# Block 2 attention: value products over both token tiles, values projected with stationary weights and turned

## Chip, cores and metric

One core of one Trainium2 chip runs the whole program in one launch. The metric is device time in microseconds (us) of that core. Three executions of the kernel before took 682.45, 682.7 and 682.95 us, median 682.7 us.

## The reference, cut to what matters

Two transformer blocks run one after the other on 256 tokens of width 1024, all in float32. The change touches only the attention of block 2: 8 query heads of 64 columns share 2 key/value heads of 64, the mask is a band of 128 tokens on both sides, there is an ALiBi bias and a sink logit per head.

```python
u = rms_norm_2(h, norm_mix[l])
proj = u @ w_in[l]
z_pool, q, k, v, g_pool, g_attn = jnp.split(proj, splits, axis=-1)
y_pool = multiscale_pool(z_pool, w_pool_group[l], pool_scale[l]) @ w_pool_branch[l]
y_attn = windowed_gqa(q, k, v, sink[l]) @ w_attn_branch[l]
...
p = (p / denom).astype(v.dtype)
out = jnp.einsum("bnhgqk,bnkhd->bnqhgd", p, vb)
```

`v` has 128 columns (2 heads of 64). `out` is the product of the probabilities with the values. After it come the branch products, a merge with two sigmoid gates, the output product, and a gated feed-forward of width 2816.

## The kernel before

Each engine has one instruction list, written out by hand, and runs it in order; the engines meet at counting semaphores (`wait_ge`, `then_inc`). Weights arrive through a ring of eight 1 MB slots by SyncE's queue. A weight slot is used in two parts: ScalarE (ACT) copies it to a rounded high part (`split_high`, line 403, two halves of 1024 columns per slot), VectorE (DVE) writes the rest (`split_low`, line 410), and a product is then three products of reduced-precision operands (`triple`, line 1622: high x high, high x low, low x high). `chunk` (line 1629) makes one 128-column slice of a projection for all 256 tokens: for each of 8 depth tiles it waits for nothing further and issues one `triple`, with the weights stationary and the 256 tokens moving, 24 products in all; before the first it waits for the low half of its slot (`split_ready`). All products are recorded on line 1614 (`mm`), all TensorE transposes on line 1617 (`turn`).

Block 2's projections run in the order pool (4 chunks), query (4 chunks), key (1 chunk, first half of slot `SPLIT1 + 4`), value (second half of that slot). The values are made by `values(i)` (line 2143), once for each of the 2 token tiles: here the 128 tokens of the tile are stationary and the 128 weight columns move, 24 products each, and the result in PSUM bank 6 has tokens on the partitions, as the value products need it. `values(0)` is called before the first scores, `values(1)` after them (line 2194). ACT's `values_out` (line 856) waits for both and copies bank 6 to `v2`, scaled by each token's reciprocal root mean square.

Then comes a loop over 16 units `u` (line 2195); `head_and_tile(u)` maps four successive units to the two heads of a pair and its two token tiles. Per unit TensorE issues: one gate chunk (two units fill PSUM bank `m % 2`, slots `SPLIT1 + 5` on, first half for even `u`), the scores of unit `u + 2` (`scores2`, 2 products), at every fourth unit the value products of the pair just finished (`values2`), and the two transposes of unit `u`'s probabilities (`turn_probs2`), which wait for `p2_done`. `values2(m, i)` makes pair `m` and token tile `i`: 4 float32 products with 128 moving columns, stationary `v2` of 64 columns, head `j` of the pair to PSUM partitions `64 j` on. Both tiles are called one after the other.

ACT's loop (line 863), for unit `u`: wait for `nm2_done`, the exponentials (lines 867 and 869), then for unit `u - 1` the copy of the turned probabilities into `pt2` (line 874), then weight splits. At `u == 0` it runs `values_out`, then `split_high(SPLIT1 + 6)`, then half of slot `SPLIT1 + 7` (lines 877 to 881).

DVE's loop (line 1505), for unit `u`: bias and row maximum of unit `u` (line 1511), then for unit `u - 1` denominator, reciprocal and scaling (lines 1518 to 1520, the last raises `p2_done`), the gate evacuation for odd `u - 1` (line 515), then weight splits: at `u == 1` it runs `split_low(SPLIT1 + 6)` and half of slot `SPLIT1 + 7`. Ahead of the loop, DVE runs `k2_low(0)` (line 509) and `split_low(SPLIT1 + 5)`.

After the loop: `values2` of the last pair, four pool products (line 2217), their evacuation on ACT (line 885) and DVE, the eight sigmoids (line 889), and a merge in which ACT and DVE take turns.

Of the kernel before, what the change touches and what calls it, by code (L numbers as in the profile page):

```python
# [21 lines left out]
ACT = mybir.ActivationFunctionType  # L22
AX = mybir.AxisListType

P = 128
D = 1024
DT = D // P
TOK = 256
NT = TOK // P
# [10 lines left out]
CT = 512 // P  # L40
# [13 lines left out]
HD = 64  # L54
# [8 lines left out]
SPLIT1 = 12  # L63
# [62 lines left out]
def two_blocks(nc, x, meta, consts, small, gains, positions, stream, out):  # L126
    ctx = ExitStack()
    with ctx:
# [62 lines left out]
        ps = ctx.enter_context(nc.psum_tensor("ps", [P, 8, 512], F32))  # L191
# [88 lines left out]
        v2 = cut(NT, 2 * HD)  # L280
# [2 lines left out]
        gate = cut(DT, 2 * TOK)  # L283
        pm2 = cut(3, TOK)
        pt2 = cut(4, TOK)
        dg2 = pt2[:, 0, :]
        u_hi, u_lo = (turned[:, j, 0:DT * TOK].rearrange("p (a b) -> p a b", b=TOK) for j in range(2))
        mg_hi, mg_lo = u_hi, u_lo

# [38 lines left out]
        s = {n: sem(n) for n in names}  # L328
# [84 lines left out]
        def split_pair(k):  # L413

            return w_hi[k % HIGHS], ring_r[:, split_slot(k)[0], :]
# [51 lines left out]
                                     mrg_hi[:, hp, :].bitcast(F32), ALU.mult, ALU.subtract).then_inc(s["att_low"], 1)  # L467

        def attention2_out(act, hp):
            act.wait_ge(s["o2_ps"], 2 * (hp + 1))  # L470
            act.activation(at_hi[:, hp, :], ps[:, 6 + hp % 2, 0:TOK], ACT.Copy).then_inc(s["o2_sb"], 1)

        def attention2_low(dve, hp):
# [23 lines left out]
        def k2_high(act, kv):  # L497
            act.wait_ge(s["q2_sb"], CT + 1)
            rows = slice(kv * HD, (kv + 1) * HD)
            for other in (kv, 1 - kv):  # L500
                act.activation(k2_split[other * HD:(other + 1) * HD, kv, :], k2T[rows, :], ACT.Copy).then_inc(s["qk_high"], 1)
# [120 lines left out]
        def _(act):  # L622
# [112 lines left out]
            for u in range(2 * HEADS + 1):  # L735
# [5 lines left out]
                if u:  # L741
                    w = u - 1
# [3 lines left out]
                    i = head_and_tile(w)[1]  # L746
# [4 lines left out]
                    if FILL <= w < FILL + 4 * NT and (w - FILL) % 2:  # L751
                        j = (w - FILL) // 2
# [100 lines left out]
            q2_high(act, 3)  # L853
            k2_high(act, 0)
            k2_high(act, 1)
            def values_out():
                act.wait_ge(s["v2_ps"], 1)
                for i in range(NT):
                    last = act.activation(v2[:, i, :], ps[:, 6, i * P:(i + 1) * P], ACT.Copy, scale=rsd[:, i:i + 1])
                last.then_inc(s["v2_sb"], 1)  # L860


            for u in range(2 * HEADS + 1):
# [7 lines left out]
                if u:  # L871
                    w = u - 1
# [739 lines left out]
        def _(pe):  # L1612
            def mm(o, lhsT, rhs, start, stop, **kw):
                return pe.matmul(o, lhsT, rhs, start=start, stop=stop, **kw)  # L1614

            def turn(o, a, rows=P):
                return pe.transpose(o, a, ident[0:rows, 0:rows])  # L1617

            def split_ready(k, half):
                pe.wait_ge(s["wlo_done"], 2 * k + half + 1)  # L1620

            def triple(o, stat_hl, mov_hl, first, last_k):

                (ah, al), (bh, bl) = stat_hl, mov_hl
                begin = mm(o, ah, bh, first, False, skip_group_check=True)
                mm(o, ah, bl, False, False, skip_group_check=True)
                return begin, mm(o, al, bh, False, last_k, skip_group_check=True)

            def chunk(o, k, half, acts, frees=0, turned_from=None, bank=0):

                split_ready(k, half)
                for t in range(DT):
                    if turned_from is not None:

                        pe.wait_ge(s["turn_dve"], turned_from + max(t, bank) + 1)
                    c = half * D + t * P
                    begin, last = triple(o, [w[:, c:c + P] for w in split_pair(k)], [a[:, t] for a in acts],
                                         t == 0, t == DT - 1)
                    if t == 0 and frees:
                        begin.then_inc(split_used, frees)  # L1640
                return last
# [23 lines left out]
            for t in range(2):  # L1665
                for i, m, c in TILES:
                    q0 = 0 if i else QL
                    w = split_pair(0)[0][:, t * ZA + q0:(t + 1) * ZA]
# [3 lines left out]
            for t in range(2):  # L1672
                for i, m, c in TILES:
                    q0 = 0 if i else QL
                    mm(ps[0:m, i, q0:ZA], x_hi[:, t, c:c + m], split_pair(0)[1][:, t * ZA + q0:(t + 1) * ZA], False, False,
                       skip_group_check=True)
            for t in range(2, DT):
                split_ready(t // 4, (t % 4) * ZA // D if t % 4 < 2 else 1)
                pe.wait_ge(s["turn_dve"], t + 1)
                for i, m, c in TILES:  # L1680
                    q0 = 0 if i else QL
                    w = [a[:, (t % 4) * ZA + q0:(t % 4 + 1) * ZA] for a in split_pair(t // 4)]
                    begin, last = triple(ps[0:m, i, q0:ZA], [x[:, t, c:c + m] for x in (x_hi, x_lo)], w, False, t == DT - 1)
# [15 lines left out]
            for i, m, c in TILES:  # L1699
                last = mm(ps[:, 6, c:c + m], ones_s[0:m, :], dg[0:m, c:c + m], True, True)  # L1700
# [6 lines left out]
            for f in range(QL // P):  # L1707
                for i in range(NT):
                    last = turn(ps[:, 1, f * TOK + i * P:f * TOK + (i + 1) * P], zt[:, 1 + i, f * P:(f + 1) * P])
            last.then_inc(s["t3_ps"], 1)  # L1710
            for i, m, c in TILES:
                last = turn(ps[:, 2, c:c + m], zt[0:m, i, QL:QL + KVL], m)
            last.then_inc(s["t3_ps"], 1)
            pe.wait_ge(s["kr_done"], 1)
            for i, m, c in TILES:
                last = turn(ps[0:QKD, 0, c:c + m], kr[0:m, i, :], m)
# [15 lines left out]
            for i in range(NT):  # L1732
# [5 lines left out]
                for b, lo, hi in ((0, 0, 512), (1, 512, HEADS * QKD)):  # L1738
                    for f in range(QL // P):
                        last = mm(ps[:, 4 + 2 * i + b, 0:hi - lo], cqT[:, f, i * P:(i + 1) * P],  # L1740
                                  ring[:, Q_SLOT, f * HEADS * QKD + lo:f * HEADS * QKD + hi], f == 0, f == QL // P - 1)
# [12 lines left out]
            for hp in range(HEADS // 2):  # L1754
                for j in range(2):
                    for i in range(NT):
                        last = turn(ps[0:QKD, qt_bank(hp), j * TOK + i * P:j * TOK + (i + 1) * P],
                                    qtok[:, i, (2 * hp + j) * QKD:(2 * hp + j + 1) * QKD])
# [32 lines left out]
            def values(m, i):  # L1791

                u = 4 * m + 2 * i
                pe.wait_ge(s["pt_sb"], u + 2)
                if m >= 2 and i == 0:

                    pe.wait_ge(s["att_low"], m - 1)
                for k in range(2 + i):
                    for j in range(2):
                        c = (2 * m + j) * VD  # L1800
                        last = mm(ps[j * VD:(j + 1) * VD, 6 + m % 2, i * P:(i + 1) * P], v1[k][:, c:c + VD],
                                  pt1[i][:, j, k * P:(k + 1) * P], i == k == 0, i == 1 and k == 1 + i, skip_group_check=True)
                last.then_inc(s["o_ps"], 1)
# [336 lines left out]
            pe.wait_ge(s["z2_sb"], 2)  # L2140
            chunk(ps[:, 0, 0:TOK], SPLIT1 + 4, 0, (u_hi, u_lo), frees=1).then_inc(s["k2_ps"], 1)

            def values(i):
                for t in range(DT):
                    begin, last = triple(ps[:, 6, i * P:(i + 1) * P], [u[:, t, i * P:(i + 1) * P] for u in (u_hi, u_lo)],
                                         [w[:, D + t * P:D + (t + 1) * P] for w in split_pair(SPLIT1 + 4)], t == 0, t == DT - 1)
                return last

            split_ready(SPLIT1 + 4, 1)
            pe.wait_ge(s["q2_sb"], 3)  # L2150
            values(0)


            def scores2(u):
                hd, i = head_and_tile(u)
                kv = hd // 4
                if u % 8 == 0:
                    pe.wait_ge(s["qk_high"], CT + 2 * kv + 2)
                    pe.wait_ge(s["qk_low"], 5 if kv else 3)
                elif u == 12:  # L2160
                    pe.wait_ge(s["qk_low"], CT + 2)
                if u >= 2:
                    pe.wait_ge(s["nm2_done"], u - 1)
                q = q2_split[:, hd, i * P:(i + 1) * P]
                mm(ps[:, 2 + u % 2, 0:TOK], q, k2_split[:, kv, :], True, False)
                mm(ps[:, 2 + u % 2, 0:TOK], q, k2_split[:, 2 + 2 * kv + hd % 2, :], False, True).then_inc(s["s2_ps"], 1)
# [6 lines left out]
                    last = turn(ps[:, 4 + u % 2, k * P:(k + 1) * P], pm2[:, u % 3, k * P:(k + 1) * P])  # L2173
                last.then_inc(s["pt2_ps"], 1)

            def values2(m, i):

                u, kv = 4 * m + 2 * i, m // 2
                pe.wait_ge(s["pt2_sb"], u + 2)
                if u == 0:  # L2180
                    pe.wait_ge(s["v2_sb"], 1)
                if m >= 2 and i == 0:
                    pe.wait_ge(s["o2_low"], m - 1)
                for k in range(NT):
                    for j in range(2):
                        last = mm(ps[j * HD:(j + 1) * HD, 6 + m % 2, i * P:(i + 1) * P], v2[:, k, kv * HD:(kv + 1) * HD],
                                  pt2[:, 2 * i + j, k * P:(k + 1) * P], i == k == 0, i == 1 and k == NT - 1, skip_group_check=True)
                last.then_inc(s["o2_ps"], 1)

            pe.wait_ge(s["q2_sb"], CT)  # L2190
            pe.wait_ge(s["z2_sb"], 5)
            scores2(0)
            scores2(1)
            values(1).then_inc(s["v2_ps"], 1)
            for u in range(2 * HEADS):
                m = u // 2
                if u % 2 == 0 and m >= 2:
                    pe.wait_ge(s["g_sb"], m - 1)
                last = chunk(ps[:, m % 2, (u % 2) * TOK:(u % 2 + 1) * TOK], SPLIT1 + 5 + m, u % 2, (u_hi, u_lo), frees=1 - u % 2)
                if u % 2:  # L2200
                    last.then_inc(s["g_ps"], 1)
                if u + 2 < 2 * HEADS:
                    scores2(u + 2)
                if u and u % 4 == 0:
                    values2(u // 4 - 1, 0)
                    values2(u // 4 - 1, 1)
                turn_probs2(u)
            values2(CT - 1, 0)
            values2(CT - 1, 1)


            for c in range(4):
# [24 lines left out]
            for k in range(DT):  # L2237
# [3 lines left out]
                for q in range(2 * NT):  # L2241
                    i, nn = q // 2, q % 2
# [218 lines left out]
```

## Time and profile before

| what | us |
|---|---|
| median of 3 executions | 682.7 (682.45 to 682.95) |
| the profiled execution, its own time | 681.71 |
| span of the profiled execution | 679.9 |
| TensorE busy (PE) | 629.5 (93% of the span) |
| DVE busy | 356.8 (52%) |
| ACT busy | 293.8 (43%) |

The profile comes from one execution. Times in its rows count from the span's start. A row of the timeline gives the start, the duration from first start to last end, the engine, the line, the operation with its tiles, the count, and in brackets the idle time just before it with what ended it. PE is TensorE's products, PEld its weight loads. Products are pipelined, so the distance between two starts is what one costs, and the duration of one also holds its way through the array. A float32 product is recorded as two products, one of reduced precision or a transpose as one. The names `turned`, `single`, `ring_r`, `work`, `extra_r` are the memory areas that hold the tiles: `turned` the tokens, `single` and `ring_r` the weights' high and low parts, `extra_r` queries and keys, `work` most else.

### The profile page before, as it was taken

To read this page: it belongs to the slowest core of one execution; us is meant where nothing else is said; L and a number is where in the kernel's file an instruction comes from. 1 tells how busy PE (TensorE), PEld (TensorE's weight loads), DVE (VectorE), ACT (ScalarE), POOL (GpSimd) and SP (SyncE) were. 2 spreads that over 40 slices of the span, in tenths; PEclk is the share of its full clock that TensorE was granted. 3 is DMA by queue.
4 is the path that set the end of the run, shared out by engine and by line. 5 is a ranking of instruction groups with operands and counts; after the bars stand their busy time and mean duration, and the time that the engine had idled before them with its cause. 6 is when DMAs were issued, how large, how long until landed. Compare 5 with 4: busy or idle time off the path is not lost.

```text
span 679.9 us, 10209 instructions
## 1 busy us (share of the span) xinstructions
PE 629.5 (93%) x4027; PEld 471.7 (69%) x4027; DVE 356.8 (52%) x689; ACT 293.8 (43%) x560; POOL 49.3 (7%) x74
## 2 busy tenths in 40 slices
PE   8999799999999766779899999999999999999996
PEld 5979677842543321334389999898788888888884
DVE  5687664831130120110088886757856666666665
ACT  6855562421111010100085765554655555555554
POOL 2100101100010000000048100000000000000001
PEclk9999999999999976979999999999999999999999
DMA  8966328989999999999997443355535555555101
GB/s 345 421 231 240 126 123 330 408 362 425 428 388 421 421 421 419 423 421 421 421 422 291 155 150 124 124 187 187 185 134 192 196 199 193 195 193 185 63 1 62
DMA packets 26286, 180.73 MB, mean 266 GB/s; under 512 B 3184, under 2 KB 3312, under 8 KB 5120
## 3 DMA queue, kind: packets, MB, share of 16 engines
q1 hardware_dynamic: 25200, 177.60, 66.1%
q10 hardware_dynamic: 1040, 2.50, 0.9%
q8 instruction: 32, 0.52, 0.3%
q14 instruction: 14, 0.11, 0.1%
HBM read 179.04 MB, written 1.05 MB: 265 GB/s over the span
## 4 chain that ended last, share of the span: by engine, by line
PE 69%; DMA 15%; DVE 8%; ACT 5%; issue 2%; POOLq 0%; SPq 0%; POOL 0%; ACTq 0%; DVEq 0%
PE ps L1614 66%; DMA ring<-stream_dram 15%; PE ps L1617 3%; DVE ring_r L410 2%; ACT single L403 1%; DVE work L1549 1%; ACT work L889 1%; DVE work L1552 1%; DVE h L1602 0%; DVE work L1605 0%; ACT turned L894 0%; ACT work_r L885 0%; DVE extra_r L509 0%; DVE work L1430 0%; ACT work L799 0%
## 5 line engine op out<-in xcount | busy, mean ns | idle before, releaser
L1614 PE MATMUL ps<-turned,single 128*128 128x256 f32 (+2 forms) x944 | 231.3, 326 | 2.6 <-ACT work L670 1.8
L1614 PE MATMUL ps<-turned,ring_r 128*128 128x256 f32 (+1 forms) x648 | 179.8, 281 | 0.0
L1614 PEld LDWEIGHTS ps<-turned,single 128*128 128x128 f32 x944 | 156.3, 189 | 19.5 <-ACT work L670 2.4
L410 DVE TENSOR_TENSOR ring_r<-ring,single 128x1024 fp32r<-128x1024 f32 (+1 forms) x132 | 160.3, 1237 | 13.6 <-ACT single L403 13.4
L403 ACT ACTIVATE single<-ring 128x1024 fp32r<-128x1024 f32 (+1 forms) x132 | 134.1, 1047 | 0.1
L1614 PEld LDWEIGHTS ps<-turned,ring_r 128*128 128x128 f32 x648 | 121.1, 188 | 0.4
L1614 PE MATMUL ps<-ring,work 128*32 128x512 f32 (+2 forms) x462 | 71.0, 621 | 16.6 <-DMA ring<-stream_dram 14.3
L1614 PE MATMUL ps<-single,turned 128*128 128x512 f32 (+3 forms) x208 | 60.2, 369 | 2.9 <-DVE turned L1229 2.2
L1614 PEld LDWEIGHTS ps<-single 128*128 128x128 f32 x257 | 38.3, 188 | 34.2 <-issue 20.8
L1614 PE MATMUL ps<-single 128*128 128x512 f32 (+1 forms) x257 | 55.2, 353 | 3.4 <-DVE single L1441 2.3
L1614 PE MATMUL ps<-single,work_r 128*128 128x512 f32 x176 | 56.2, 392 | 0.0
L1614 PEld LDWEIGHTS ps<-ring,work 128*32 128x32 f32 (+1 forms) x462 | 19.9, 120 | 49.8 <-issue 23.2
L1582 DVE TENSOR_TENSOR work<-work,ps 128x512 f32<-128x512 f32 x22 | 15.1, 688 | 60.0 <-ACT work L919 59.8
L919 ACT ACTIVATE work<-ps 128x512 f32<-128x512 f32 x22 | 13.2, 598 | 73.1 <-PE ps L1614 73.1
L1614 PEld LDWEIGHTS ps<-single,turned 128*128 128x128 f32 (+1 forms) x208 | 36.7, 183 | 10.5 <-issue 2.5
L806 ACT ACTIVATE work<-ps 128x256 f32<-128x256 f32 x8 | 3.1, 384 | 91.6 <-PE ps L1614 91.6
L1614 PE MATMUL ps<-work 128*64 128x128 f32 (+7 forms) x272 | 38.8, 373 | 2.6 <-DVE work L1087 1.8
L1430 DVE TENSOR_TENSOR work<-work,ps 128x256 f32<-128x256 f32 x8 | 3.4, 422 | 70.4 <-ACT work L806 70.4
L1441 DVE SCALAR_TENSOR_TENSOR single<-ps,work,single 128x512 fp32r<-128x512 f32 x16 | 12.0, 751 | 52.7 <-ACT single L812 52.7
L1614 PEld LDWEIGHTS ps<-single,work_r 128*128 128x128 f32 x176 | 33.0, 187 | 7.3
L1614 PE MATMUL ps<-ring,turned_w 128*32 128x512 f32 x208 | 30.1, 688 | 8.0 <-DMA ring<-stream_dram 5.8
L1614 PE MATMUL ps<-ring_r,turned 128*128 128x512 f32 (+3 forms) x104 | 36.9, 363 | 0.0
(260 smaller groups left out, 703.6 us busy)
## 6 DMA issues: line engine op xcount, KB each, us to landing
ring<-stream_dram SPq DMA_DIRECT2D x145, 1024.0 KB, 11.9
work<-stream_dram SPq DMA_DIRECT2D x12, 1024.0 KB, 12.3
turned_w<-stream_dram SPq DMA_DIRECT2D x4, 1024.0 KB, 14.0
extra<-stream_dram SPq DMA_DIRECT2D x2, 1024.0 KB, 11.6
ring<-stream_dram SPq DMA_DIRECT2D x2, 832.0 KB, 7.6
h<-x_dram SPq DMA_DIRECT2D x2, 512.0 KB, 4.6
gain<-gains_dram ACTq DMA_DIRECT2D x2, 512.0 KB, 10.4
yields<-stream_dram SPq DMA_DIRECT2D x1, 1024.0 KB, 12.3
```

What stands on the lines that cost most here:

```text
L403: act.activation(w_hi[k % HIGHS][:, a], ring[:, place, a], ACT.Copy).then_inc(s["whi_done"], 1)
L410: dve.tensor_tensor(ring_r[:, place, a], ring[:, place, a], w_hi[k % HIGHS][:, a].bitcast(F32), ALU.subtract).then_inc(s["wlo_done"], 1)
L806: act.activation(sg, ps[:, 4, 0:FF], ACT.Silu).then_inc(s["sg_done"], 1)
L889: act.activation(gate[:, m, :], gate[:, m, :], ACT.Sigmoid).then_inc(s["sig_done"], 1)
L919: act.activation(fpart[:, m % 2, :].rearrange("p (a b) -> p a b", b=TOK), ffn_banks(m)[:, :, TOK:2 * TOK], ACT.Copy).then_inc(s["fsg_done" ...
L1430: dve.tensor_tensor(htok, sg, ps[:, 4, FF:2 * FF], ALU.mult).then_inc(s["ht_done"], 1)
L1441: dve.scalar_tensor_tensor(yl[:, n * 512:(n + 1) * 512], ps[:, 6 + n, :], wsl[:, p:p + 1], yh[:, n * 512:(n + 1) * 512].bitcast(F32), ALU. ...
L1549: dve.tensor_tensor(gate[:, m, :], gate[:, m, :], ps[:, 2 + m % 4, :], ALU.mult).then_inc(s["br_sb"], 1)
L1552: dve.tensor_tensor(gate[:, m, 0:TOK], gate[:, m, 0:TOK], gate[:, m, TOK:2 * TOK], ALU.add).then_inc(s["mg_sum"], 1)
L1582: dve.tensor_tensor(halves(fsum[:, m % 2, :], TOK), halves(fpart[:, m % 2, :], TOK), ffn_banks(m)[:, :, 0:TOK], ALU.add).then_inc(s["fh_su ...
L1614: return pe.matmul(o, lhsT, rhs, start=start, stop=stop, **kw)
L1617: return pe.transpose(o, a, ident[0:rows, 0:rows])
```

## The change

The values are made like every other chunk: weights stationary, 256 tokens moving, 24 products into PSUM bank 1. The result has the value columns on the partitions. ACT copies it, unscaled, to `v2_turned` (the fourth quarter of `pt2`, free until unit 3). TensorE turns it with two transposes into bank 6 (`values_turned`), and from there `values_out` goes on as before. `values_turned` stands in unit 0 of the loop, behind the gate chunk and the scores of unit 2. `values2(m)` takes both token tiles in one product: 4 products per pair with 256 moving columns (two stretches of 128 in `pt2`) in place of 8 with 128, and one wait for all four units of the pair.

```diff
--- before.py
+++ after.py
@@ -283,7 +283,7 @@
         gate = cut(DT, 2 * TOK)
         pm2 = cut(3, TOK)
         pt2 = cut(4, TOK)
-        dg2 = pt2[:, 0, :]
+        dg2, v2_turned = pt2[:, 0, :], pt2[:, 3, :]
         u_hi, u_lo = (turned[:, j, 0:DT * TOK].rearrange("p (a b) -> p a b", b=TOK) for j in range(2))
         mg_hi, mg_lo = u_hi, u_lo
 
@@ -467,7 +467,7 @@
                                      mrg_hi[:, hp, :].bitcast(F32), ALU.mult, ALU.subtract).then_inc(s["att_low"], 1)
 
         def attention2_out(act, hp):
-            act.wait_ge(s["o2_ps"], 2 * (hp + 1))
+            act.wait_ge(s["o2_ps"], hp + 1)
             act.activation(at_hi[:, hp, :], ps[:, 6 + hp % 2, 0:TOK], ACT.Copy).then_inc(s["o2_sb"], 1)
 
         def attention2_low(dve, hp):
@@ -853,8 +853,10 @@
             q2_high(act, 3)
             k2_high(act, 0)
             k2_high(act, 1)
+            act.wait_ge(s["v2_ps"], 1)
+            act.activation(v2_turned, ps[:, 1, 0:TOK], ACT.Copy).then_inc(s["v2_sb"], 1)
             def values_out():
-                act.wait_ge(s["v2_ps"], 1)
+                act.wait_ge(s["v2_ps"], 2)
                 for i in range(NT):
                     last = act.activation(v2[:, i, :], ps[:, 6, i * P:(i + 1) * P], ACT.Copy, scale=rsd[:, i:i + 1])
                 last.then_inc(s["v2_sb"], 1)
@@ -2140,16 +2142,15 @@
             pe.wait_ge(s["z2_sb"], 2)
             chunk(ps[:, 0, 0:TOK], SPLIT1 + 4, 0, (u_hi, u_lo), frees=1).then_inc(s["k2_ps"], 1)
 
-            def values(i):
-                for t in range(DT):
-                    begin, last = triple(ps[:, 6, i * P:(i + 1) * P], [u[:, t, i * P:(i + 1) * P] for u in (u_hi, u_lo)],
-                                         [w[:, D + t * P:D + (t + 1) * P] for w in split_pair(SPLIT1 + 4)], t == 0, t == DT - 1)
-                return last
-
-            split_ready(SPLIT1 + 4, 1)
-            pe.wait_ge(s["q2_sb"], 3)
-            values(0)
-
+            pe.wait_ge(s["z2_sb"], 3)
+            chunk(ps[:, 1, 0:TOK], SPLIT1 + 4, 1, (u_hi, u_lo)).then_inc(s["v2_ps"], 1)
+
+            def values_turned():
+                pe.wait_ge(s["v2_sb"], 1)
+                pe.wait_ge(s["q2_sb"], 3)
+                for i in range(NT):
+                    last = turn(ps[:, 6, i * P:(i + 1) * P], v2_turned[:, i * P:(i + 1) * P])
+                last.then_inc(s["v2_ps"], 1)
 
             def scores2(u):
                 hd, i = head_and_tile(u)
@@ -2173,25 +2174,24 @@
                     last = turn(ps[:, 4 + u % 2, k * P:(k + 1) * P], pm2[:, u % 3, k * P:(k + 1) * P])
                 last.then_inc(s["pt2_ps"], 1)
 
-            def values2(m, i):
-
-                u, kv = 4 * m + 2 * i, m // 2
-                pe.wait_ge(s["pt2_sb"], u + 2)
-                if u == 0:
-                    pe.wait_ge(s["v2_sb"], 1)
-                if m >= 2 and i == 0:
+            def values2(m):
+
+                kv = m // 2
+                pe.wait_ge(s["pt2_sb"], 4 * (m + 1))
+                if m == 0:
+                    pe.wait_ge(s["v2_sb"], 2)
+                if m >= 2:
                     pe.wait_ge(s["o2_low"], m - 1)
                 for k in range(NT):
                     for j in range(2):
-                        last = mm(ps[j * HD:(j + 1) * HD, 6 + m % 2, i * P:(i + 1) * P], v2[:, k, kv * HD:(kv + 1) * HD],
-                                  pt2[:, 2 * i + j, k * P:(k + 1) * P], i == k == 0, i == 1 and k == NT - 1, skip_group_check=True)
+                        last = mm(ps[j * HD:(j + 1) * HD, 6 + m % 2, 0:TOK], v2[:, k, kv * HD:(kv + 1) * HD],
+                                  pt2[:, j:4:2, k * P:(k + 1) * P], k == 0, k == NT - 1, skip_group_check=True)
                 last.then_inc(s["o2_ps"], 1)
 
             pe.wait_ge(s["q2_sb"], CT)
             pe.wait_ge(s["z2_sb"], 5)
             scores2(0)
             scores2(1)
-            values(1).then_inc(s["v2_ps"], 1)
             for u in range(2 * HEADS):
                 m = u // 2
                 if u % 2 == 0 and m >= 2:
@@ -2201,12 +2201,12 @@
                     last.then_inc(s["g_ps"], 1)
                 if u + 2 < 2 * HEADS:
                     scores2(u + 2)
+                if u == 0:
+                    values_turned()
                 if u and u % 4 == 0:
-                    values2(u // 4 - 1, 0)
-                    values2(u // 4 - 1, 1)
+                    values2(u // 4 - 1)
                 turn_probs2(u)
-            values2(CT - 1, 0)
-            values2(CT - 1, 1)
+            values2(CT - 1)
 
 
             for c in range(4):
```

## Rows read from the trace of the kernel before

**Rows 1.** Busy time of each engine by stretch (us), granted clock, DMA.

```profile
core 0: us, PE busy (x) PEld busy (x) DVE busy (x) ACT busy (x) POOL busy (x), PEclk, DMA share, GB/s
...
388.00:440.00 52.00, 51.57 (x456) 49.90 (x455) 39.78 (x101) 30.09 (x73) 0.00 (x0) 1.00 0.40 142
...
476.60:679.90 203.30, 196.50 (x1036) 168.18 (x1036) 131.34 (x180) 107.83 (x163) 4.08 (x12) 0.99 0.42 150
```

**Rows 2.** Chain that ended last, in order of time: start, us, what.

```profile
443.29 3.74 ACT work L889 x7
...
490.38 179.19 PE ps L1614 x954
```

**Rows 3.** Timeline of TensorE, 374 to 388: values, scores, first gate chunks.

```profile
374.73 0.22 PE L1614 MATMUL ps<-single,turned 128*128 128x128 f32 x1
...
377.78 0.71 PE L1614 MATMUL ps<-extra_r 128*128 128x256 f32 x4 [0.26 <-DVE extra_r L509]
378.33 0.22 PE L1614 MATMUL ps<-single,turned 128*128 128x128 f32 x1
...
380.96 0.45 PE L1614 MATMUL ps<-turned,single 128*128 128x256 f32 x2
...
383.87 0.40 PE L1614 MATMUL ps<-extra_r 128*128 128x256 f32 x2
384.10 0.39 PE L1617 MATMUL ps<-cst,work 128*128 128x128 f32 x2
384.25 0.48 PE L1614 MATMUL ps<-turned,single 128*128 128x256 f32 x2
...
387.43 0.38 PE L1617 MATMUL ps<-cst,work 128*128 128x128 f32 x2
```

**Rows 4.** Timeline of ACT, 377 to 385.

```profile
377.15 1.28 ACT L867 ACT_TABLE_LOAD   x1
...
380.98 0.28 ACT L869 ACTIVATE stat<-vec,stat 128x1 f32<-128x1 f32 x1
381.16 0.62 ACT L859 ACTIVATE work<-ps,stat 128x128 f32<-128x128 f32 x2
381.67 2.95 ACT L403 ACTIVATE single<-ring 128x1024 fp32r<-128x1024 f32 x3
```

**Rows 5.** Timeline of DVE, 377 to 388.

```profile
377.67 2.36 DVE L410 TENSOR_TENSOR ring_r<-ring,single 128x1024 fp32r<-128x1024 f32 x2
...
381.68 0.35 DVE L1520 TENSOR_SCALAR work<-work,stat 128x256 f32<-128x256 f32 x1
382.76 3.50 DVE L410 TENSOR_TENSOR ring_r<-ring,single 128x1024 fp32r<-128x1024 f32 x3 [0.73 <-ACT single L403]
...
386.97 0.35 DVE L1520 TENSOR_SCALAR work<-work,stat 128x256 f32<-128x256 f32 x1
...
389.93 0.35 DVE L1520 TENSOR_SCALAR work<-work,stat 128x256 f32<-128x256 f32 x1
```

**Rows 6.** Timeline of TensorE: value products of two pairs, then the pool products.

```profile
426.95 1.09 PE L1614 MATMUL ps<-work 128*64 128x128 f32 x16
427.97 0.44 PE L1617 MATMUL ps<-cst,work 128*128 128x128 f32 x2
...
437.80 1.20 PE L1614 MATMUL ps<-work 128*64 128x128 f32 x16
438.93 1.99 PE L1614 MATMUL ps<-work,vec 128*128 128x256 f32 x8
```

**Rows 7.** Timeline of ACT: copy of the last unit's turned probabilities.

```profile
437.91 0.38 ACT L874 ACTIVATE work<-ps 128x256 f32<-128x256 f32 x1 [1.74 <-PE ps L1617]
```

**Rows 8.** Busy time by stretch (columns of Rows 1), in block 1.

```profile
80.10:83.50 3.40, 0.92 (x6) 0.74 (x7) 2.26 (x8) 3.40 (x10) 0.73 (x1) 1.00 0.47 128
83.50:86.90 3.40, 3.40 (x10) 2.72 (x11) 1.51 (x7) 0.72 (x4) 0.00 (x0) 0.50 1.02 426
```

**Rows 9.** Timeline of TensorE in block 1, around 83.

```profile
83.38 0.64 PE L1614 MATMUL ps<-single,turned 128*128 128x512 f32 x1 [2.17 <-DVE turned L1229]
```

## The prediction

> **What bounds the kernel now.** I read the busy time by stretch first, then the chain that ended last, then the timelines of the three engines around unit 0, where the change acts. In the 52 us of the loop over units TensorE is busy for 51.57 us, DVE for 39.78, and from 476.6 to the end TensorE again for 196.5 of 203.3 us [rows 1]. The chain shows the feed-forward as one piece of 179 us on TensorE, and between loop and feed-forward a stretch in which ACT's sigmoids and the merge are on it [rows 2]: none of that touches the change, and DMA is busy for only four tenths [rows 1]. So a microsecond won or lost on TensorE in the loop should reach the end, unless ACT or DVE delivers late. That second condition decides here.
>
> **Values, on TensorE.** Before, 24 products with 128 columns run from 374.73, and 24 more from 378.33 to 380.96 [rows 3]: 2.63 us, 0.110 each. A chunk with 256 columns starts at 380.96 and its scores at 383.87: 2.91 us, 0.12 each [rows 3]. Halving the columns hardly made a product cheaper, so 48 become 24 and TensorE loses 2 x 2.63 = 5.26 and gains 2.9 us of work, plus two transposes (0.15 us from 384.10 to 384.25 [rows 3]): 2.2 us less. None of the first half is won: the new chunk ends at 374.73 + 2.9 = 377.6, and the scores start at 377.78 as before, since DVE's key split releases them [rows 3]. At 378.33 TensorE comes to the gate chunk, where `values(1)` stood. That chunk waits for the low half of slot `SPLIT1 + 5`, which DVE begins at 377.67; two halves take 2.36 us, one about 1.22 [rows 5], so it is there at 378.89. With 0.14 us to the first product (the lag that the scores show: DVE's key split ends at about 377.65) the chunk starts at 379.03, not at 380.96. So 1.9 us are in hand, and 0.7 were spent in a wait that `values(1)` had covered.
>
> **Values, on ACT.** The new copy of 256 columns (0.38 us by the copy of the same shape [rows 7]) starts when the values chunk has left the array, about 377.8; ACT has nothing then but a table load, and TensorE wants the copy at 382.2. Cost nothing; with no cover it would be 0.4 us plus a second load of 1.28 [rows 4]. But `values_out` now waits for `values_turned`, which stands behind gate chunk and scores: 379.03 + 2.91 + 0.23 (scores, 383.87 to 384.10 [rows 3]) = 382.17, two transposes, out of the array at 382.55, ACT at 382.6. Before, the two copies of `values_out` started at 381.16, straight behind the exponential's last instruction [rows 4]. They move by **1.44 us**, and in ACT's queue three weight copies (line 403) stand behind them [rows 4].
>
> **The wait that takes its place.** DVE already waits 0.73 us for the first of these copies, then runs three splits in 3.50 us, then unit 1's scaling, done at 386.97 + 0.35 = 387.32 [rows 5]. Unit 1's transposes start at 387.43, only 0.11 later [rows 3]. With 1.44 us on the copies unit 1's probabilities are done at 388.76 and the transposes start at about 388.81. TensorE comes there much sooner: unit 0's transposes at 382.4 (their input is done at 382.03 [rows 5]), the chunk at 382.55, and 3.18 us from chunk to transposes (384.25 to 387.43 [rows 3]) give 385.7. So it idles for about 3 us and goes on **1.38 us later** than before. Next in line is unit 2: its scaling would end at 389.93 + 0.35 + 1.44 = 391.72 [rows 5], TensorE needs it at 388.81 + 3.33 = 392.14 (387.43 less 384.10 is one unit [rows 3]); it holds, and the lag is carried along. Bounds: if the gate chunk didn't have to wait for its low half, ACT would be late by 0.74 and TensorE by 0.7; if every handover costs 0.1 more, 1.7.
>
> **Value products.** For one pair 16 records of 128 columns take 1.02 us (426.95 to 427.97), although a lone record of 256 columns takes 0.249 (8 in 1.99 us) [rows 6]: 16 times half of that would be 1.99. So the two heads' products, which write different halves of the partitions, run beside each other. With 256 columns 8 records in 4 such pairs stream what 16 did: I take 1.02 again, 0 gained. Lower end 4 x 0.22 = 0.88 (0.14 less), upper end 8 x 0.249 = 1.99 (0.97 more per pair, if they no longer run side by side). The value taken is that of the nearest row, same operands and shape of weights. The Trainium skill ("TensorEngine Tiling (Array Packing)", section "Instruction Overhead") gives every product an overhead of about 60 cycles; 16 fewer would save an estimated 0.4 us at 2.4 GHz, and the sum would be 685.5. The rows don't show it here.
>
> **The last pair.** Before, tile 0 of the last pair ran while ACT copied unit 15's probabilities, done at 437.91 + 0.38 = 438.29 [rows 7], and the pool products began at 438.93 [rows 6]. Now all four products wait for that copy: start 438.34, 1.02 us, pool products at 439.36. That is **0.43 us** later; ACT's evacuation, the sigmoids and the merge hang on it. Bounds 0.3 and 1.4 (the two ends above).
>
> **The clock.** Before, TensorE never rests for 3 us in this stage. In block 1 it did 0.92 us of work between 80.1 and 83.5, with an idle time of 2.17 us at the end [rows 8, 9]; from 83.5 to 86.9 its granted clock was 0.50, 1.2 instead of 2.4 GHz, then full again under steady work [rows 8]. The new wait is longer, so I expect the same once: 3.4 us at half speed cost at most 1.7 us, nothing if the level holds. Part of that stretch may lie inside the wait or beside DVE's slack of 0.4 us; I take **1.4**.
>
> **Sum.** 1.38 + 0.43 + 0 + 1.4 = 3.2 us. Against the profiled execution's 681.71 that is 684.9; its time lies 1.0 below the median of the runs, so the forecast is 682.7 + 3.2 = **685.9**.
>
> **The rivals.**
> *The wait comes, the clock stays full:* 1.38 + 0.43 = 1.8, 684.5. For it: a clock that fell once, in another stage with other products, is thin evidence. Against it: the idle time is longer than the one that was followed by the fall.
> *TensorE's gain gets through (not slower):* the place is unit 1's transposes. If ACT's first weight copy is there when DVE has scaled unit 0, at 382.03, DVE goes on without a wait, and the 4.56 us from its three splits' start to unit 1's scaling (382.76 to 387.32 [rows 5]) end at 386.6. TensorE is then 0.8 us ahead from there on, still held by DVE, and pays 0.43 at the end: -0.4, 682.3, and 681.9 if the end hides too. It decides at whether that copy, of about 1 us, starts by 381.0; the code puts it behind `values_out`, at 383.1.
> *The value products lose their side-by-side running:* 4 x 0.97 = 3.9 on top of 1.8, 688.4. Nothing in the rows speaks for it but the new moving operand of two stretches.
> *The lags are smaller than I work out and the clock stays:* 0.7 + 0.3 = 1.0, 683.7, inside 0.2% (1.4 us), which is about what a measurement of this kernel can tell from no change.
>
> **How the numbers follow.** Forecast 0.50, wait without the clock 0.27, gain gets through 0.08, products apart 0.04, smaller lags 0.11. The range goes from 683.5, below the second case and with most of the last, to 687.0 (the upper bounds of wait and clock: 1.7 + 0.43 + 1.7 + some tenths); outside lie the gain and the products apart, with parts of the others. Slower by over 0.2% holds the forecast, the products apart and nearly all of the second case: 0.79. Within 0.2%: the smaller lags and most of the gain's case, 0.17. Faster by over 0.2%: 0.04, if that case has more in it than I find.
>
> **What would show it.** Right: one idle time of 2.5 to 3 us ahead of line 1617, released by DVE's line 1520, with `values_out` on ACT at about 382.6 and DVE's wait for line 403 about 2.2 us instead of 0.73; products of 256 columns with 64 weights at about 0.25 us per two; a clock under 1.00 in the stretch behind the wait. Wrong: no such idle time, or the pool products at or before 438.93 on the span; then DVE had more slack than I count.

## The result, and the profile after

The changed kernel takes 685.15 us (median of 12 runs, 684.07 to 686.86), the kernel before 683.0 us beside it (12 runs, 682.1 to 684.6): ratio 1.003, 95% interval 1.0018 to 1.0041. It is slower by 2.15 us, 0.3%. The profiled execution took 684.46 us with a span of 682.7; TensorE is busy for 627.1 us, 2.4 less than before.

Block 1 doesn't take the same time in every execution: the first scores of block 2 started between 377.78 and 382.33 us in the profiles of this study. So I compare stretches that begin at the first scores, the four products with `extra_r` of units 0 and 1 (377.78 before [rows 3], 378.86 after). What releases them is DVE's key split, before and after:

```profile
375.91 1.73 DVE L509 TENSOR_TENSOR extra_r<-work,extra_r 64x256 fp32r<-64x256 f32 x2 [0.55 <-ACT extra_r L501]
```

```profile
376.96 1.75 DVE L509 TENSOR_TENSOR extra_r<-work,extra_r 64x256 fp32r<-64x256 f32 x2 [0.56 <-ACT extra_r L501]
```

It starts 1.87 us ahead of the scores before and 1.90 after, so the new value chunk in front of them neither gains nor costs there. From the start of the pool products to the end of the span every profile of this study takes 240.8 to 241.0 us, so what is late there is late at the end. Helper lines are two higher after: 1616 for products, 1619 for transposes, 1522 for the last step of DVE's scaling. In the runs in which the splits are spread, further down, products are on line 1615 and transposes on line 1618.

TensorE's timeline of the changed kernel, with the first gate chunk, the transposes of values and unit 0 together, unit 1's transposes, and the value products of the last two pairs:

```profile
378.86 0.71 PE L1616 MATMUL ps<-extra_r 128*128 128x256 f32 x4
380.03 0.50 PE L1616 MATMUL ps<-turned,single 128*128 128x256 f32 x2 [0.46 <-DVE ring_r L410]
...
383.23 0.60 PE L1619 MATMUL ps<-cst,work 128*128 128x128 f32 x4
...
389.87 0.44 PE L1619 MATMUL ps<-cst,work 128*128 128x128 f32 x2 [2.95 <-DVE work L1522]
...
429.46 1.08 PE L1616 MATMUL ps<-work 128*64 128x256 f32 x8
430.47 0.44 PE L1619 MATMUL ps<-cst,work 128*128 128x128 f32 x2
...
440.87 1.08 PE L1616 MATMUL ps<-work 128*64 128x256 f32 x8 [0.47 <-ACT work L876]
441.88 1.99 PE L1616 MATMUL ps<-work,vec 128*128 128x256 f32 x8
```

The one new line that matters is the idle time of 2.95 us ahead of unit 1's transposes. They start 389.87 - 378.86 = 11.01 us behind the first scores; before it was 387.43 - 377.78 = 9.65 [rows 3]. So 48 products of 128 columns became 24 of 256, and TensorE is 1.36 us later. The pool products start 441.88 - 378.86 = 63.02 us behind the first scores, before 438.93 - 377.78 = 61.15 [rows 6]: 0.51 us have been added to the 1.36 by then. Each pair's value products take 1.01 us (429.46 to 430.47), 1.02 before [rows 6].

What TensorE waits for is read backwards. The chain that ended last runs through it:

```profile
383.39 0.24 PE ps L1619 x2
...
383.92 0.36 ACT work L861
384.28 0.96 ACT single L403
385.23 0.02 issue
385.26 3.50 DVE ring_r L410 x3
388.75 0.40 DVE work L1513
...
389.46 0.37 DVE work L1522
389.83 0.04 issue
389.87 0.44 PE ps L1619 x2
```

The turned values (383.39) release ACT's `values_out`, which now stands on line 861; behind it comes the weight copy, then DVE's three splits, then unit 1's scaling. Before, the chain stayed on TensorE in this stretch:

```profile
377.78 6.49 PE ps L1614 x54
384.27 0.22 PE ps L1617 x2
384.49 3.10 PE ps L1614 x26
387.59 0.22 PE ps L1617 x2
```

After the change the timelines of ACT and DVE give the sizes:

```profile
379.24 1.28 ACT L869 ACT_TABLE_LOAD   x1
...
382.06 0.28 ACT L871 ACTIVATE stat<-vec,stat 128x1 f32<-128x1 f32 x1
383.65 0.63 ACT L861 ACTIVATE work<-ps,stat 128x128 f32<-128x128 f32 x2 [1.31 <-PE ps L1619]
384.17 2.95 ACT L403 ACTIVATE single<-ring 128x1024 fp32r<-128x1024 f32 x3
```

```profile
382.76 0.35 DVE L1522 TENSOR_SCALAR work<-work,stat 128x256 f32<-128x256 f32 x1
385.26 3.50 DVE L410 TENSOR_TENSOR ring_r<-ring,single 128x1024 fp32r<-128x1024 f32 x3 [2.14 <-ACT single L403]
...
389.46 0.35 DVE L1522 TENSOR_SCALAR work<-work,stat 128x256 f32<-128x256 f32 x1
```

ACT waits 1.31 us for the turned values, and DVE 2.14 us for ACT's first copy instead of 0.73 [rows 5].

### The profile page after: what moved, and what is told of

Same layout as the page of the kernel before. It is cut to its first block, busy times and chain, and to the rows that moved or that the text cites. A ratio compares the mean times of both kernels' runs of the same rounds, so it can differ in the third digit from the quotient of the medians.

```text
span 682.7 us, 10103 instructions
## 1 busy us (share of the span) xinstructions
PE 627.1 (92%) x3973; PEld 467.9 (69%) x3973; DVE 357.0 (52%) x689; ACT 294.6 (43%) x561; POOL 49.4 (7%) x74
## 4 chain that ended last, share of the span: by engine, by line
PE 68%; DMA 15%; DVE 9%; ACT 5%; issue 2%; POOLq 0%; SPq 0%; POOL 0%; ACTq 0%; DVEq 0%
PE ps L1616 65%; DMA ring<-stream_dram 15%; PE ps L1619 3%; DVE ring_r L410 3%; ACT single L403 1%; DVE work L1551 1%; ACT work L891 1%; DVE work L1554 1%; DVE h L1604 0%; DVE work L1607 0%; ACT turned L896 0%; ACT work_r L887 0%; DVE extra_r L509 0%; DVE work L1432 0%; ACT work L799 0%
## 5 line engine op out<-in xcount | busy, mean ns | idle before, releaser
L1616 PE MATMUL ps<-turned,single 128*128 128x256 f32 (+2 forms) x960 | 234.2, 326 | 3.0 <-ACT work L670 1.8
L1616 PE MATMUL ps<-turned,ring_r 128*128 128x256 f32 (+1 forms) x656 | 182.0, 281 | 0.0
L1616 PEld LDWEIGHTS ps<-turned,single 128*128 128x128 f32 x960 | 158.8, 189 | 20.2 <-ACT work L670 2.4
L1616 PEld LDWEIGHTS ps<-turned,ring_r 128*128 128x128 f32 x656 | 122.6, 188 | 0.4
L1616 PE MATMUL ps<-single,turned 128*128 128x512 f32 (+2 forms) x176 | 54.5, 387 | 2.9 <-DVE turned L1231 2.1
L1616 PEld LDWEIGHTS ps<-single,turned 128*128 128x128 f32 (+1 forms) x176 | 31.5, 181 | 10.3 <-issue 2.5
L1025 POOL TENSOR_SCALAR stat<-stat 128x1 f32<-128x1 f32 (+1 forms) x7 | 4.7, 666 | 439.4 <-ACT ps L936 177.6
L1616 PE MATMUL ps<-ring,turned_w 128*32 128x512 f32 x208 | 27.8, 641 | 9.3 <-DMA ring<-stream_dram 6.7
```

Of the source, the lines that this page charges most:

```text
L1025: pool.tensor_scalar(ms, ss, 1.0 / D, EPS, ALU.mult, ALU.add).then_inc(s["pool_step"], 1)
```

## The experiments

Each kernel ran 12 times beside the kernel before on the same chip, in four groups. The kernel before ran 12 times in the first group (the result) and 35 times in each of the others; its medians were 683.0, 683.50, 683.51 and 683.83 us. The ratio and its interval are worked out from all executions of a group, so the ratio is not exactly that of the two medians. The columns in the middle are worked out from starts in each run's one profile as above, in us behind the first scores.

| kernel | unit 1's transposes | pool products | median us | ratio to before, 95% interval |
|---|---|---|---|---|
| before | 9.65 | 61.15 | 683.0 to 683.83 | |
| changed | 11.01 | 63.02 | 685.15 | 1.0030 (1.0018 to 1.0041) |
| changed, again | 11.00 | 62.98 | 685.11 | 1.0026 (1.0014 to 1.0038) |
| values alone | 11.01 | 65.34 | 686.44 | 1.0039 (1.0023 to 1.0055) |
| values alone, again | 11.01 | 62.62 | 684.96 | 1.0024 (1.0012 to 1.0036) |
| value products alone | 9.62 | 61.59 | 683.19 | 1.0001 (0.9984 to 1.0017) |
| turn early | 9.57 | 61.56 | 683.34 | 1.0001 (0.9987 to 1.0014) |
| filler in the wait | 11.00 | 62.98 | 684.56 | 1.0028 (1.0013 to 1.0043) |
| values alone, filler | 11.02 | 62.61 | 684.60 | 1.0009 (0.9995 to 1.0024) |
| DVE's splits spread alone | 9.76 | 61.75 | 684.12 | 1.0010 (0.9998 to 1.0021) |
| turn early, splits spread | 8.33 | 60.31 | 681.99 | 0.9986 (0.9972 to 1.0000) |
| the same, last pair by tiles | 8.33 | 59.89 | 682.31 | 0.9979 (0.9968 to 0.9990) |
| the same, ACT spread too | 7.68 | 59.19 | 681.16 | 0.9963 (0.9950 to 0.9976) |
| before, with both spreads | 9.65 | 61.24 | 683.65 | 1.0004 (0.9991 to 1.0016) |

**The two parts, each alone.** First the values in the new way, with `values2(m, i)` as before:

```diff
-                    values2(u // 4 - 1)
+                    values2(u // 4 - 1, 0)
+                    values2(u // 4 - 1, 1)
```

> Only the values are made in the new way (stationary weights, copied, turned); the value products keep their two token tiles. Theory (ACT's copies of the turned values stand ahead of its weight copies, DVE's splits and unit 1's transposes come late): the idle time of about 2.95 us ahead of unit 1's transposes stays, TensorE goes on 1.36 us later than before, the pool products carry that lag and nothing more: about 1.4 us above the kernel before, up to 1.7 more if the clock falls behind the wait. Rival (the value products over 256 columns cost the time): no more than 0.2 us above the kernel before.

Then the value products over both tiles, with the values as before (`values(0)`, `values(1)`):

```diff
-                    values2(u // 4 - 1, 0)
-                    values2(u // 4 - 1, 1)
+                    values2(u // 4 - 1)
```

> Only the value products take both token tiles at once; the values are made as before. Theory: 16 records of 128 columns in 1.02 us become 8 of 256 in about 1.02, no gain in the loop, and the last pair waits for the copy of the last unit: pool products 0.45 to 0.5 us later, time 0.5 us above the kernel before. Rival (the value products cost the time): 2 us above.

TensorE's timeline of the second, at the last pair:

```profile
438.71 1.08 PE L1614 MATMUL ps<-work 128*64 128x256 f32 x8 [0.47 <-ACT work L874]
439.72 1.99 PE L1614 MATMUL ps<-work,vec 128*128 128x256 f32 x8
```

The parts separate as expected. The value products alone move nothing up to unit 1 (9.62) and cost 0.44 us at the end, where all of them wait for the last copy; before, eight of the sixteen records ran in that wait [rows 6, 7]. The time of whole executions can't resolve 0.44 us here. The values alone bring the whole lag of 1.36 us. In the profile of the first run there was more, pool products at 65.34 instead of 61.15 + 1.36 = 62.5, and the busy time by stretch with TensorE's timeline says why:

```profile
379.00:389.30 10.30, 7.61 (x60) 7.23 (x60) 7.63 (x15) 7.81 (x15) 0.00 (x0) 1.00 0.30 104
389.30:396.10 6.80, 6.05 (x29) 6.05 (x30) 5.41 (x15) 2.90 (x8) 0.00 (x0) 0.50 0.42 154
```

```profile
390.05 0.69 PE L1619 MATMUL ps<-cst,work 128*128 128x128 f32 x2 [2.94 <-DVE work L1522]
390.39 0.78 PE L1616 MATMUL ps<-turned,single 128*128 128x256 f32 x2
...
395.66 0.63 PE L1616 MATMUL ps<-extra_r 128*128 128x256 f32 x2
```

From 389.3 to 396.1 the granted clock (the column behind the five engines) is 0.50, and a gate chunk takes 395.66 - 390.39 = 5.27 us instead of the 2.91 of before [rows 3]. It fell while TensorE still waited: the transposes start at 390.05. The same kernel with the clock full has its pool products at 62.62 ("values alone, again"): the fall cost 2.72 us.

**The order of the turn.** The changed kernel with the two transposes ahead of unit 0's gate chunk:

```diff
             scores2(0)
             scores2(1)
+            values_turned()
...
-                if u == 0:
-                    values_turned()
```

> As the changed kernel, but the two transposes of the values stand ahead of unit 0's gate chunk, straight behind the scores of units 0 and 1. Theory: values_out starts behind the first exponential again, DVE's wait for line 403 falls from 2.14 to about 0.7 us, the idle time ahead of unit 1's transposes from 2.95 to about 1.75 us; they start where they did before, so 1.4 us less than the changed kernel and 0.5 us more than the kernel before. Rival (the gate chunk that waits for its low half behind DVE's key split makes the lag): that wait is as it was, so no change against the changed kernel.

DVE's wait, then TensorE's two, in the timelines of this run:

```profile
384.71 3.50 DVE L410 TENSOR_TENSOR ring_r<-ring,single 128x1024 fp32r<-128x1024 f32 x3 [0.71 <-ACT single L403]
```

```profile
380.91 0.50 PE L1616 MATMUL ps<-turned,single 128*128 128x256 f32 x2 [0.23 <-DVE ring_r L410]
...
389.32 0.44 PE L1619 MATMUL ps<-cst,work 128*128 128x128 f32 x2 [1.74 <-DVE work L1522]
```

DVE's wait is back at 0.71 us, the transposes are where they were before (9.57), and the pool products are 0.41 us late, by the last pair. That shows the place of the turn to be the cause of the lag. The rival falls, since the gate chunk waits for its low half here as well and starts 380.91 - 379.75 = 1.16 us behind the first scores, as in the changed kernel (1.17). TensorE still rests for 1.74 us: its gain is there, but DVE has no earlier probabilities for it.

**Is it the clock?** The changed kernel, and later the values alone, with 22 products into an unused bank during the wait:

```diff
+                if u == 1:
+                    idle_products(ps[:, 7, 0:TOK], split_pair(SPLIT1 + 5)[0][:, 0:P], u_hi[:, 0, :], 22)
                 turn_probs2(u)
```

> As the changed kernel, but TensorE makes 22 products of 256 columns into an unused bank (about 2.6 us) ahead of unit 1's transposes, so that it works through the wait. Theory with the clock (behind the wait the granted clock falls in a part of the executions): all executions come near the lower ones of the changed kernel, 684.4 us, and the median falls by 0.7. Rival (the clock has no part in it): median and spread as the changed kernel, 685.2 us. If the filler itself delayed the transposes, both would be above that.

> The changed kernel again, for the granted clock behind its wait of about 2.95 us. Theory: in a part of the executions it falls to 0.50 for 3.4 to 6.8 us within 4 us of the wait, at a price of up to 2.8 us (what the profile of the values alone shows between first scores and pool products: 65.34 against 62.5 without), so times stand about 684.4 where it holds and 686 to 687 where it falls. Rival (that fall belonged to the other kernel): 1.00 there, times as the kernel before plus 1.8 us with its spread.

> The values alone, with 22 products of 256 columns into an unused bank in the wait ahead of unit 1's transposes, so that TensorE rests for 0.3 us instead of 2.94. Theory (the clock fell behind that wait in most executions of the values alone): granted clock 1.00 behind it, median 684.9 (before plus 1.4) instead of 686.4, at most a sixth of the executions above 685.5 where 9 of 12 were. Rival (the extra time above 1.4 us has another cause): median stays near 686.4.

> The values alone again, on the chip and beside the runs of the one with the filler. Theory: more than half of the executions above 685.5 as before, and a granted clock of 0.50 within 4 us of the wait in the profile if that execution is one of them; pool products 62.5 us behind the first scores where it holds, 65.3 where it falls for 6.8 us. Rival: as the run with the filler.

```profile
385.86 2.81 PE L1616 MATMUL ps<-turned,single 128*128 128x256 f32 x22
388.97 0.44 PE L1619 MATMUL ps<-cst,work 128*128 128x128 f32 x2 [0.30 <-DVE work L1522]
```

In the profile of the filled wait (above) the filler fits and delays nothing: 11.00 and 62.98, as without it. On the clock the answer is partial. Of the four profiles with the open wait of 2.95 us (changed, changed again, values alone, values alone again) one shows the fall. Neither of the two of the changed kernel does; the row of the first, for the 6.8 us from the end of the wait on:

```profile
389.90:396.70 6.80, 6.80 (x58) 6.80 (x59) 5.87 (x16) 4.32 (x11) 0.00 (x0) 1.00 0.42 154
```

Whole executions don't decide how often it falls. Above 685.5 us were 6 and 4 of 12 of the changed kernel, 9 and 4 of 12 of the values alone, but also 4 and 3 of 12 with the filler, and the kernel before scatters by some us itself (681.8 to 686.52 in the last group). The slowest execution with the filler, 687.62 us, is the profiled one: its clock is 1.00 all through the loop, and its first scores start at 382.33 us, 4.55 later than in the profile of the kernel before. So a time above 685.5 is no sign of a fall. The first run of the values alone was also on another chip than its repetition and the run with its filler. My expectations of "all executions come near the lower ones", "more than half" and "at most a sixth" failed; side by side the two medians were 684.96 open and 684.60 filled. That the clock can fall at this wait, and for what price, is seen in one execution; that the wait is its cause isn't shown, and its share of the 2.15 us stays open.

**What holds unit 1.** DVE's splits, one per unit instead of three in unit 1, with the turn where the change has it:

```diff
-                if u == 1:
-                    split_low(dve, SPLIT1 + 6)
...
-                    split_low_half(dve, SPLIT1 + 7 + (u - 1) // 2, (u - 1) % 2)
+                    for n in ((u - 1,) if u < 9 else (u - 1, u) if u == 9 else (u,) if u < 13 else (u, u + 1) if u == 13 else (u + 1,)):
+                        split_low_half(dve, SPLIT1 + 6 + n // 2, n % 2)
```

> As the changed kernel, the turn of the values where the change has it, with DVE's splits spread alone. Theory: DVE still waits 2.1 us for ACT's first copy, but only one split stands between that and unit 1's probabilities: idle time ahead of the transposes about 0.9 us instead of 2.95, transposes 8.8 us behind the first scores, time 0.4 us below the kernel before, and no fall of the clock behind the wait. Rival (ACT's copies alone hold it): idle time stays above 2 us.

and the same with the early turn:

> As the run with the early turn, and DVE spreads its weight splits: one half of slot SPLIT1 + 6 in unit 1 (instead of three halves), then one half per unit, two in units 9 and 13. Theory (in the new order DVE's queue, and nothing on TensorE, holds unit 1's transposes): DVE has unit 1's probabilities some 2.3 us sooner, no idle time over 0.3 us ahead of the transposes, which start 7.7 us behind the first scores (9.65 before, 11.0 changed); with 0.44 us lost at the last pair 1.5 us below the kernel before. Rival (the splits are needed that early, or DVE is short all through the loop): a new wait in units 2 to 6 gives it back, time as the kernel before or above.

DVE's timeline of the spread alone, then that of early turn and spread, each with the row of TensorE's timeline at unit 1's transposes:

```profile
386.18 1.23 DVE L410 TENSOR_TENSOR ring_r<-ring,single 128x1024 fp32r<-128x1024 f32 x1 [2.15 <-ACT single L403]
...
388.74 0.16 DVE L1520 TENSOR_TENSOR stat<-stat 128x1 f32<-128x1 f32 x1 [0.93 <-ACT stat L871]
```

```profile
389.55 0.44 PE L1618 MATMUL ps<-cst,work 128*128 128x128 f32 x2 [1.71 <-DVE work L1522]
```

```profile
383.60 1.23 DVE L410 TENSOR_TENSOR ring_r<-ring,single 128x1024 fp32r<-128x1024 f32 x1 [0.71 <-ACT single L403]
...
386.17 0.16 DVE L1520 TENSOR_TENSOR stat<-stat 128x1 f32<-128x1 f32 x1 [0.94 <-ACT stat L871]
```

```profile
386.97 0.44 PE L1618 MATMUL ps<-cst,work 128*128 128x128 f32 x2 [0.49 <-DVE work L1522]
```

The transposes move the way expected, but less far: to 9.76 and 8.33 instead of 8.8 and 7.7, and TensorE still waits 1.71 and 0.49 us ahead of them instead of 0.9 and at most 0.3. I had overlooked a second wait. With one split instead of three DVE comes 0.93 us too early to unit 1's exponentials, which stand behind ACT's own three weight copies. So two queues are loaded ahead of unit 1, and relieving one moves the wait to the other. The spread alone doesn't make the change a gain: I expected 0.4 us below the kernel before, and the pool products are 0.60 us later. With the early turn they are 61.15 - 60.31 = 0.84 us earlier; the 1.5 us that I expected stand in the medians (683.51 - 681.99 = 1.52), but the interval reaches 1.0000, so that agreement says little.

**A version that beats both.** Early turn and spread splits, the last pair by tiles as before, then ACT's copies spread too:

> As the run with early turn and spread splits, and the last pair's value products by token tiles as before, so that one tile runs while the last unit is copied. Theory: the 0.44 us of the last pair come back too, 1.9 us below the kernel before (pool products 59.2 us behind the first scores, 61.15 before). Rival (that tail is hidden behind ACT): as the run without it.

```diff
-                    split_high(act, SPLIT1 + 6)
-                if u < 2 * HEADS:
-                    split_high_half(act, SPLIT1 + 7 + u // 2, u % 2)
+                if u < 2 * HEADS:
+                    for n in ((0,), (1, 2), (3, 4))[u] if u < 3 else (u + 2,):
+                        split_high_half(act, SPLIT1 + 6 + n // 2, n % 2)
```

> As the run with early turn, spread splits and the last pair by tiles, and ACT too makes one weight copy (not three) ahead of unit 1's exponentials, two in units 1 and 2. Theory (there DVE waited 0.94 us for unit 1's exponentials, which stood behind ACT's three copies): that wait goes, transposes of unit 1 start 7.75 us behind the first scores (8.33 without), pool products 59.3 behind them (59.89 without, 61.15 before), time 1.8 us below the kernel before. Rival (another wait in the loop takes it): pool products stay at 59.9.

> The kernel before with the same spread of ACT's copies and DVE's splits and nothing of the change. Theory: TensorE did not wait at unit 1's transposes before (they started 0.11 us behind their input), so it gains nothing: transposes 9.6 us behind the first scores, pool products 61.1, time as the kernel before within 0.3 us. Rival (the spread alone is what gains in the other runs): 1 us or more below the kernel before.

ACT's, then TensorE's timeline of the last version:

```profile
383.39 1.05 ACT L403 ACTIVATE single<-ring 128x1024 fp32r<-128x1024 f32 x1
384.33 0.50 ACT L869 ACTIVATE work<-work,stat 128x256 f32<-128x256 f32 x1
```

```profile
379.51 0.71 PE L1615 MATMUL ps<-extra_r 128*128 128x256 f32 x4
...
387.19 0.39 PE L1618 MATMUL ps<-cst,work 128*128 128x128 f32 x2
...
438.70 1.99 PE L1615 MATMUL ps<-work,vec 128*128 128x256 f32 x8
```

Unit 1's exponentials follow one copy, the transposes start without an idle time, 7.68 us behind the first scores, and the pool products are 1.96 us earlier than in the kernel before. The median is 681.16 us beside 683.83: ratio 0.9963. That is 2.67 us; the interval, about 1.6 to 3.4 us, holds the 1.96. The last pair by tiles brings back 60.31 - 59.89 = 0.42 us in the profile; whole executions don't show it (681.99 without, 682.31 with it), and the 59.2 expected of that run came only with ACT's spread. The spreads without the change gain nothing (9.65, 61.24): TensorE had no wait there to lose, so the gain is the change's own, once the queues let it through. It is all there at unit 1 (9.65 - 7.68 = 1.97 us), ahead of the first value products, so it comes from the values and not from the merged products.

## Why the prediction was right, and where its sum was off

The direction, the range (683.5 to 687.0) and the mechanism held, but for the clock; the size was 3.2 us forecast and 2.15 measured. That 685.9 looks near to 685.15 is in part luck: the kernel before took 683.0 us beside the changed one, 0.3 more than the 682.7 that the forecast starts from. Of the signs named ahead all were there but the last, the clock. Step by step:

- *Values, on TensorE.* The gate chunk was forecast 1.25 us behind the first scores (379.03 - 377.78) and started 380.03 - 378.86 = 1.17 behind them, held by DVE's split as said. The ACT copy ahead of the loop cost nothing.
- *Values, on ACT.* `values_out` forecast 1.44 us later; measured (383.65 - 378.86) - (381.16 - 377.78) = 1.41.
- *The wait that takes its place.* Idle time forecast at about 3 us, measured 2.95; lag 1.38 forecast, 1.36 measured; unit 2 held, as said. The early turn and the values alone show the late turn to be the cause.
- *Value products.* 1.02 us forecast, 1.01 measured, with two-stretch operands: the two heads go on running beside each other (1.01 / 4 = 0.25 us per two; no row gives the 0.22 of my lower end). The estimate of 0.4 us saved by 16 fewer products at about 60 cycles each, from the Trainium skill ("TensorEngine Tiling (Array Packing)", section "Instruction Overhead"), is not borne out: it would be 0.1 us per pair, and the rows show 0.01.
- *The last pair.* 0.43 forecast; 0.44 in the run of the products alone, 0.51 in the changed kernel. From the first pair's value products to the pool products both lose 0.43 (41.48 us before, 41.91 in both); the other 0.08 of the changed kernel lies between unit 1's transposes and the first pair's value products (397.45 - 387.43 = 10.02 us before, 399.97 - 389.87 = 10.10 after).
- *The clock.* This is the mis-sized term: "so I expect the same once", priced at 1.4 us. In both profiles of the changed kernel the clock stayed at 1.00 behind the wait. In one of four profiles with this wait it fell, and then for 6.8 us at 2.72 us, not for 3.4 at 1.4. My upper bound of 1.7 was too low for it as well: with 1.8 for the rest it gives 682.7 + 4.5 = 687.2, outside the range. A fall that comes in some executions belongs into the range, not into the sum; the case I had second ("the wait comes, the clock stays full", 684.5) is the one that the profile shows. Its 1.8 us agree with 63.02 - 61.15 = 1.87. The median's 2.15 and the 1.6 of the second comparison (685.11 less 683.51) lie on both sides of it; the first interval, 1.2 to 2.8 us, holds it, so the runs neither need a share of falls nor rule one out.
- *The gain gets through.* The condition that I gave, ACT's first copy there when DVE has scaled unit 0, was met in no run: even with the early turn DVE waited 0.71 us for that copy, as before, and TensorE started unit 1 only 0.08 us sooner. I had not seen the other way to the gain, less work behind that copy: with the early turn, DVE's spread alone starts unit 1's transposes 1.32 us sooner than before, ACT's spread too 1.97.

## What to carry to other kernels

Before a step is moved down one engine's list, look at what stands behind its consumer on the next engine: here 1.4 us on a small copy reached TensorE through weight copies and splits that the change doesn't touch. Fewer products on the busiest engine are worth only as much as the engines that feed it can keep up with. Where a list has a knot (here three splits or copies in one unit, one in the others), spreading it can let the gain through; here it did so together with the early turn, and alone it gained nothing. A wait in which an engine used to have its own other work (half of a pair's products) is no longer free when that work is merged behind it.

## What the runs showed of the hardware that was not expected

At the same idle time of 2.94 us on TensorE the granted clock fell to 0.50 for 6.8 us in one execution of a kernel and stayed at 1.00 in another of the same kernel, on another chip: the fall is not a property of the program alone. And the value products of a pair of heads, float32 with 64 weight columns, take 1.01 us as 4 products of 256 columns and 1.02 as 8 of 128: neither the number of instructions nor the two-stretch operand shows.
